# A hybrid decoder block on Trainium2: GpSimd makes the second half of a weight tile's low part, and the last three tiles run bank by bank

## The reference

```
q = xn @ w_query
v1, i1 = top_k(scores with the first 128 keys, 16)
v2, i2 = top_k(scores with the second 128 keys, 16)
best, pos = top_k(all 256 sums of v1 and v2, 16)
experts = e1 * 128 + e2; gates = softmax(best)
a = gelu(xn . expert_u[experts]) * gates
out = sum over the token's 128 experts of a * expert_v[experts]
```

## Time and profile before

| what | value |
|---|---|
| median of 3 runs | 1667.56 us (1667.17 to 1668.67) |
| the profiled execution | 1666.98 us |
| its span, first to last instruction | 1665.2 us |
| granted clock of TensorE, mean | 0.999 |
| TensorE busy (as drawn) | 1653.1 us, 99% |
| VectorE busy | 1291.1 us, 78% |
| ACT busy | 678.3 us, 41% |
| GpSimd busy | 309.5 us, 19% |

### The profile page before, as it was taken

How to read it: one execution, slowest core, us unless ns; L and a number is a source line. 1 busy time by engine, 2 the same in 40 slices (tenths; PEclk the granted TensorE clock), 3 DMA queues, 4 the chain that set the end, 5 groups by cost and what they waited for, 6 DMA issues and landing times.

```text
span 1665.2 us, 25994 instructions
## 1 busy us (share of the span) xinstructions
PE 1653.1 (99%) x8965; PEld 1467.0 (88%) x8965; DVE 1291.1 (78%) x2298; ACT 678.3 (41%) x897; POOL 309.5 (19%) x267
## 2 busy tenths in 40 slices
PE   9999999999999999999999999999999999999998
PEld 7888888888889999999999999998888888888886
DVE  6855633335549999998999998676788988898886
ACT  5332433334335333344665656433343333333333
POOL 0000000000000100012222222341223433343330
PEclk9999999999999999999999999999999999999999
DMA  4323323223223676579998999996999999999993
GB/s 172 124 97 101 114 100 101 90 99 102 101 89 102 219 229 213 193 232 334 317 323 321 323 339 335 362 396 231 323 351 380 374 406 372 383 397 366 396 341 143
DMA packets 122164, 415.88 MB, mean 250 GB/s; under 512 B 13696, under 2 KB 16768, under 8 KB 120448
## 3 DMA queue, kind: packets, MB, share of 16 engines
q1 hardware_dynamic: 75168, 232.85, 39.5%
q0 software_dynamic: 36864, 134.23, 22.3%
q10 hardware_dynamic: 10080, 48.24, 7.3%
HBM read 366.77 MB, written 48.50 MB: 249 GB/s over the span
## 4 chain that ended last, share of the span: by engine, by line
PE 86%; DVE 10%; issue 3%; DMA 0%; ACT 0%; DVEq 0%; SPq 0%; ACTq 0%
PE bank L835 16%; PE bank L837 16%; PE bank L836 16%; PE bank L996 10%; PE bank L997 10%; PE bank L995 10%; PE bank L977 4%; DVE w_lo L1049 1%; DVE less L1317 1%; DVE top_i L1324 1%; DVE rows L1414 1%; DVE top_i L1316 1%; DVE top_v L1321 1%; DVE top_v L1313 1%; DVE found L1380 1%
## 5 line engine op out<-in xcount | busy, mean ns | idle before, releaser
L1049 DVE TENSOR_TENSOR w_lo<-w_raw,w_hi 128x1024 fp32r<-128x1024 f32 x347 | 423.9, 1221 | 203.0 <-ACT w_hi L538 192.0
L538 ACT ACTIVATE w_hi<-w_raw 128x1024 fp32r<-128x1024 f32 x347 | 366.5, 1057 | 441.4 <-PE bank L997 305.8
L835 PE MATMUL bank<-xn_hi,w_hi 128*128 128x384 f32 (+1 forms) x1472 | 522.7, 355 | 3.2 <-DVE w_lo L1049 3.2
L837 PE MATMUL bank<-xn_hi,w_lo 128*128 128x384 f32 (+1 forms) x1472 | 517.0, 351 | 0.0
L836 PE MATMUL bank<-xn_lo,w_hi 128*128 128x384 f32 (+1 forms) x1472 | 516.9, 351 | 0.0
L500 POOL DMA_INDIRECT rows<-u_rows,expert x128 | 144.3, 1127 | 1051.8 <-DVE expert L1440 544.1
L995 PE MATMUL bank<-w_hi,a_hi 128*128 128x512 f32 x768 | 298.8, 389 | 0.0
L996 PE MATMUL bank<-w_lo,a_hi 128*128 128x512 f32 x768 | 298.8, 389 | 0.0
L997 PE MATMUL bank<-w_hi,a_lo 128*128 128x512 f32 x768 | 298.8, 389 | 0.0
L835 PEld LDWEIGHTS bank<-xn_hi,w_hi 128*128 128x128 f32 x1472 | 276.4, 188 | 21.7 <-issue 4.6
L837 PEld LDWEIGHTS bank<-xn_hi,w_lo 128*128 128x128 f32 x1472 | 276.3, 188 | 17.6
(11 more groups left out here) (200 smaller groups left out, 1380.0 us busy)
## 6 DMA issues: line engine op xcount, KB each, us to landing
w_raw<-u SPq DMA_DIRECT2D x128, 512.0 KB
w_raw<-v SPq DMA_DIRECT2D x128, 512.0 KB
g_dram<-g_sb ACTq DMA_DIRECT2D x12, 2048.0 KB
g_in<-g_dram SPq DMA_DIRECT2D x84, 256.0 KB
act_dram<-act_out ACTq DMA_DIRECT2D x54, 384.0 KB
act_in<-act_dram SPq DMA_DIRECT2D x54, 384.0 KB
w_raw<-gate SPq DMA_DIRECT2D x32, 512.0 KB
w_raw<-w_in SPq DMA_DIRECT2D x31, 512.0 KB
```

What stands on the lines that cost most here:

```text
L538: act.activation(w_hi[:, slot, :], w_raw[:, slot, :], ACT.Copy).then_inc(hi_done, 1)
L835: pe.matmul(out, hi, x_hi, start=k == 0, stop=False)
L837: last = pe.matmul(out, lo, x_hi, start=False, stop=k == NB - 1)
L1049: dve.tensor_tensor(w_lo[:, slot, :], w_raw[:, slot, :], w_hi[:, slot, :].bitcast(F32), ALU.subtract).then_inc(lo_done, 1)
```

## The change

For the 48 `u` tiles from AT_U + 4 to AT_U + 51, those whose `w_lo` VectorE makes in the steps 0 to 11 of the search, VectorE subtracts only the first 512 of the 1024 columns and counts `lo_done`. GpSimd subtracts the other 512 (`upper_rest`) as soon as `hi_done` allows, and counts `upper_lo`, which starts at 8. TensorE waits for `upper_lo` in the middle of such a tile, ahead of its fifth block. SP's load of a tile into a slot that held such a tile waits for `upper_lo` as well. GpSimd's queue gets the subtractions in the order of the steps: four for step 0 ahead of the first gathers, then four for each step, with three gathers behind those of an even step; the other gathers come after step 11. TensorE's loop over the steps is cut in two: a loop over the halved ones, and one step written out. At the end, FINAL_TILES is 3: the last group does one tile whole and three bank by bank.

```diff
--- before.py
+++ after.py
@@ -111,6 +111,9 @@
 G_FIRST = (2 * SLOTS - 1, SLOTS)
 
 
+HALVED_AT, HALVED_END = AT_U + SLOTS, AT_U + SLOTS * (TOPK_STEPS + 1)
+
+
 USES_GATE = NB
 USES_OUT = USES_GATE + NB
 USES_QUERY = USES_OUT + NB // SLOTS
@@ -124,7 +127,7 @@
 
 
 V_BANK = (6, 4, 0, 2)
-FINAL_TILES = 2
+FINAL_TILES = 3
 
 
 def g_spans(block):
@@ -338,6 +341,7 @@
         half_loaded, half_hi, half_lo = sem("half_loaded"), sem("half_hi"), sem("half_lo")
         hi_done = sem("hi_done")
         lo_done = sem("lo_done")
+        upper_lo = sem("upper_lo")
         job_done = sem("job_done")
         bank_free = [sem(f"bank_free{b}") for b in range(SLOTS)]
         consts = sem("consts")
@@ -400,10 +404,12 @@
 
         @block.sync
         def _(sp):
-            def load_raw(source, k, n, slot):
+            def load_raw(source, k, n, slot, halved=False):
 
                 if not isinstance(n, int) or n >= SLOTS:
                     sp.wait_ge(lo_done, n - SLOTS + 1)
+                if halved:
+                    sp.wait_ge(upper_lo, k + 1)
                 sp.dma_start(w_raw[:, slot, :], source[ds(k), :, :].rearrange("o p d -> (o p) d")
                              ).then_inc(raw_loaded[slot], 16)
 
@@ -437,7 +443,10 @@
                                  ).then_inc(g_loaded[block % 2], 16)
                     at += end - begin
 
-            load_all(u_d, AT_U, KEYS - N_PIECES)
+            load_all(u_d, AT_U, HALVED_AT + SLOTS - AT_U)
+            for e2 in range(HALVED_AT + SLOTS - AT_U, HALVED_END + SLOTS - AT_U):
+                load_raw(u_d, e2, AT_U + e2, e2 % SLOTS, halved=True)
+            load_all(u_d, AT_U, KEYS - N_PIECES, start=HALVED_END + SLOTS - AT_U)
             for k in range(2):
                 sp.wait_ge(g_stored[k], 16 * N_PIECES // 2)
             for piece in range(N_PIECES):
@@ -502,13 +511,35 @@
                                         in_offset=bass.IndirectOffsetOnAxis(ap=expert[:, r:r + 1], axis=0)
                                         ).then_inc(rows_loaded[slot], 16)
 
-            pool.wait_ge(experts_ready, 1)
-            pool.wait_ge(x_turned, 2)
-            for r in range(PAIRS):
+            def upper_rest(step, b):
+
+                pool.wait_ge(hi_done, AT_U + SLOTS * (step + 1) + b + 1)
+                pool.tensor_tensor(w_lo[:, b, HALF:], w_raw[:, b, HALF:], w_hi[:, b, HALF:].bitcast(F32),
+                                   ALU.subtract).then_inc(upper_lo, 1)
+
+            def gather_u(r):
                 if r >= ROW_SLOTS:
                     pool.wait_ge(rows_used, r - ROW_SLOTS + 1)
                 pool.sem_inc(wait_carried, 1)
                 gather(u_rows, r, r % ROW_SLOTS)
+
+            pool.sem_inc(upper_lo, 2 * SLOTS)
+            for b in range(SLOTS):
+                upper_rest(0, b)
+            pool.wait_ge(experts_ready, 1)
+            pool.wait_ge(x_turned, 2)
+            gathered = ROW_SLOTS
+            for r in range(gathered):
+                gather_u(r)
+            for step in range(1, TOPK_STEPS):
+                for b in range(SLOTS):
+                    upper_rest(step, b)
+                if step % 2 == 0:
+                    for r in range(gathered, gathered + DOTS_TOPK):
+                        gather_u(r)
+                    gathered += DOTS_TOPK
+            for r in range(gathered, PAIRS):
+                gather_u(r)
             for r in range(PAIRS):
                 if r < ROW_SLOTS:
                     pool.wait_ge(rows_used, PAIRS - ROW_SLOTS + r + 1)
@@ -816,7 +847,7 @@
                 return tensor[:, slot, k * P:(k + 1) * P]
 
             def tile_product(n, b, uses, act_hi, act_lo, parts=None, base=0, tokens=slice(0, T), used=None,
-                             halves=False):
+                             halves=False, halved=None):
 
 
                 if halves:
@@ -827,6 +858,8 @@
                 for k in range(NB):
                     if halves and k == NB // 2:
                         pe.wait_ge(lo_done, n + 1)
+                    if halved is not None and k == NB // 2:
+                        pe.wait_ge(upper_lo, halved)
                     if parts is not None:
                         pe.wait_ge(parts, base + k + 1)
                     hi, lo = k_block(w_hi, b, k), k_block(w_lo, b, k)
@@ -941,12 +974,16 @@
                 last.then_inc(x_turned, 1)
             score(last_group, SLOTS - 1)
 
-            def u_tile(step, b, parts=None):
-                tile_product(SLOTS * step + (AT_U + b), b, step + (USES_U + 1), xn_hi, xn_lo, parts, NB, tokens=DENSE)
+            def u_tile(step, b, parts=None, halved=None):
+                tile_product(SLOTS * step + (AT_U + b), b, step + (USES_U + 1), xn_hi, xn_lo, parts, NB, tokens=DENSE,
+                             halved=halved)
 
             for b in range(SLOTS):
                 u_tile(0, b, xn_l if b == 0 else None)
-            with pe.Fori(1, ONEHOT_AT - 1) as step:
+            with pe.Fori(1, TOPK_STEPS + 1) as step:
+                for b in range(SLOTS):
+                    u_tile(step, b, halved=SLOTS * step + (SLOTS + b + 1))
+            for step in range(TOPK_STEPS + 1, ONEHOT_AT - 1):
                 for b in range(SLOTS):
                     u_tile(step, b)
             for b in range(SLOTS // 2):
@@ -1043,10 +1080,10 @@
             chain = Chain(dve, dve_step)
             norms = [0]
 
-            def split_weight(n, slot):
+            def split_weight(n, slot, columns=slice(0, D)):
 
                 dve.wait_ge(hi_done, n + 1)
-                dve.tensor_tensor(w_lo[:, slot, :], w_raw[:, slot, :], w_hi[:, slot, :].bitcast(F32),
+                dve.tensor_tensor(w_lo[:, slot, columns], w_raw[:, slot, columns], w_hi[:, slot, columns].bitcast(F32),
                                   ALU.subtract).then_inc(lo_done, 1)
 
             def inverse_rms(sums, columns):
@@ -1298,7 +1335,8 @@
             def u_split(step, b):
                 dve.wait_ge(act_ready, SLOTS * step + (b + 1))
                 dve.sem_inc(bank_free[b], 1)
-                split_weight(SLOTS * step + (AT_U + SLOTS + b), b)
+                n = SLOTS * step + (AT_U + SLOTS + b)
+                split_weight(n, b, slice(0, HALF if HALVED_AT <= n < HALVED_END else D))
 
             def search(c, i, at, splits):
```

## The result

| | before | after |
|---|---|---|
| median | 1667.37 us (6 runs) | 1677.86 us (6 runs) |
| lowest and highest | 1667.07 and 1668.67 | 1676.93 and 1678.23 |
| the profiled execution | 1666.98 us | 1677.62 us |
| its span | 1665.2 us | 1675.8 us |

The ratio is 1.006, with a 95% interval of 1.0047 to 1.0073: **slower by 10.5 us**, where 4.5 us off had been forecast.

A forecast was written before the change was run, and what follows sets the result against it. VectorE was taken to bound the search, costing TensorE 4.2 us of waits. 4.2 + 0.4 (tail) - 0.1 (loop restart) = 4.5 us off the 1667.56 us median gave 1663.0 us, range 1662.0 to 1668.5.

The forecast's parts named there:

- What bounds the kernel: Search stretch: TensorE loses 4.2 us waiting for VectorE's w_lo; VectorE needs 34.62 us a period, TensorE 33.26.
- Part 1: VectorE's w_lo subtraction halved for 48 tiles: 0.53 us saved a tile; 4.2 us of TensorE waits go.
- Part 2: Other half of w_lo on GpSimd: 1.2 us each, with 12.9 us of room for lateness; costs nothing.
- Parts 3 and 4: New waits cost nothing, TensorE's loop restart loses 0.1 us; last three tiles bank by bank gain nothing to 0.4 us.
- rival 1: Search: VectorE is held up by GpSimd's subtractions; slower, 1697.5 us if the full 1.16 us were lost each time; chance 0.13.
- half is 0.24, below 0.44: VectorE's hold: a 1.16 us subtraction meets 0.47 us of two-input instructions; half is 0.24; up to 0.44 no wait.
- The lead of 3.9 us: VectorE's lead in the search: it loses 8.2 us over six periods, 4.2 show as waits, so 3.9 us of lead.

The follow-up runs named there:

- the first experiment: Changed kernel with GpSimd waiting and counting but subtracting nothing, low part of the second half of 48 tiles left out: 1662.94 us, ratio 0.9973.
- the two runs told when to start: Changed kernel, gathers in odd steps, GpSimd's subtractions signalled by VectorE at one-input runs: 1665.6 us; with that signal also awaiting the last dot: 1664.32 us.

## Why the prediction was wrong

- **What bounds the kernel: right.** 4.2 us of waits, VectorE short in the search; with it relieved, the kernel took 1662.9 us and TensorE ran at pace. That agrees with the 1663.0 forecast for that case.
- **Part 1, right without GpSimd.** The half takes 682 ns as drawn, where the whole took 1214; by VectorE's busy time (1291.1 and 1266.7 us) 0.51 us a tile were saved in the first experiment.
- **Part 2, the length right, the cost wrong.** GpSimd's subtraction has a minimum of 1.26 and a median of 1.30 us, where 1.2 was put, and was never late for TensorE. That it "costs nothing" named what covers GpSimd, and left what it takes from VectorE to the rival. This is where the sum should have had a term. The Trainium skill's figure (GPSIMD Engine Reference, section 3.1, a quarter of 4497 ns) comes to 1.12 us, an estimate 0.14 to 0.18 us below the rows here.
- **Parts 3 and 4, right.** No wait of TensorE in mid-tile; 0.37 us off at the end. The 0.1 us put down for the loop's restart doesn't show: no interval of the first experiment's search is over pace.
- **The step that failed** is in rival 1: "half is 0.24, below 0.44". Measured is 0.70. It multiplied the share of two-input time with GpSimd's length, as if the two ran independently, and halved it. Three things were wrong in that. The subtractions don't lie evenly: behind the gathers they stand in rows of two or three, and one VectorE instruction waits for a whole row. That was 12.7 of 33.7 us, and spreading took 11.5 away. The chance to be held isn't the share of time either: a GpSimd instruction that begins in a one-input stretch still holds the next two-input instruction for what is left of it, as `cand` (273 to 739 ns) shows, which stands behind long one-input runs. And being first doesn't halve the loss: the half at 658.72 is drawn from ahead of GpSimd's row and was held to its end, and in sum GpSimd waited some 5.8 us where VectorE waited 33.7. Where GpSimd does wait, it takes the next turn, as with the dots at 577 us. That these last two explain all of the 0.46 us that stay when the rows are gone is argued, not shown.
- **The price of rival 1 was right in kind.** Its balance, 0.53 us a tile at which nothing changes, gives (0.70 - 0.53) x 48 = 8 us slower, less 0.4 at the end; 10.5 were measured. That these lie so near is in part luck: the waits themselves grew by 6.2 us, less than the 8, and 4.0 us came from the clock, which the formula left out. The lead of 3.9 us isn't to be relied on either: at 0.46 us a tile it leaves 1 us of waits, and the run with the gathers spread had 4.4, the first of them at 571 us, when the lead should have been whole. Held instructions come in lumps, and a lead summed over a period doesn't cover a lump.
- **Where the two-input rule stood.** The Trainium skill (SBUF — State Buffer, "Who interferes with whom") was named beside rival 1 as speaking for it. The rows agree: two-input instructions held, write-only fills harmless (682 ns), MAX8 and FIND_INDEX8 untouched, and the cast with one input held twice (0.77 and 1.26 us instead of 0.29), which that page lists as an operation that can take the second port. The prediction's "for the whole instruction" is what the page says of VectorE's two-port modes; of the shared ports in general it says "an exclusive lock". The rows show such a hold for two SBUF inputs as well (585.67: to the end of the third subtraction). That the hold's "size lies with who starts first", which the prediction took from the rule, isn't borne out by the starts as drawn (658.72). Rival 1 got a chance of 0.13, from the product above; with a hold that lasts whole instructions the count should have started at that end.

## What to carry to other kernels

Work given to GpSimd beside a busy VectorE had a price on VectorE here (0.16 to 0.70 us a piece) that is counted by meetings: for each GpSimd instruction that reads SBUF, look in VectorE's order at which two-input instruction comes next, and take the whole rest of the GpSimd instruction, and of any queued straight behind it, as lost. Keep such work behind a signal that VectorE gives at the start of a one-input run, keep it out of rows behind waits, or, cheaper, look first for VectorE work that can be moved to a later stretch. Where it is moved to matters as much as that it is moved: with five dots in front of the first masks, where their rows weren't there in time, the kernel was 4.9 us slower than before, with them in later steps 2.5 us faster.

## What was not expected of the hardware

- GpSimd's queued subtractions aren't interleaved with a waiting VectorE instruction: a half given out in the first of three ran after the third (3.49 us). With dots queued on VectorE, turns were taken. What decides between the two wasn't tried.
- A copy on GpSimd (0.62 us, one input) cost VectorE 0.16 us a tile, a subtraction of a quarter (0.74 us) 0.20, and one of a half (1.30 us) 0.70; the loss grew faster than the length.
- Gathers by themselves held up no two-input instruction that could be seen (halves at 682 ns and dots at 1219 in the first experiment, with 23 gathers among them), but a cast beside a gather took 0.39 to 0.53 us instead of 0.29, in the two runs told when to start.
- TensorE's granted clock fell where 3.8 us lay between two starts (605.87 and 680.07 us) and where 7.8 did (the masks in the run with the early dots): 0.32 us a matmul, the 1.2 GHz level, for up to 6 us (609.7 to 615.6). Where 1.4 us lay between two starts it stayed at the 2.4 GHz level, three times in the kernel before. A longer wait so costs more than its length.
